# Two branch products in three fp32r passes, with group norm's factors applied ahead of its root

## The reference, cut to what matters

```python
# end of rwkv7_mix: group norm over 64 channels, weight, bias, bonus, gate
y = ((y - mean) * lax.rsqrt(var + GN_EPS)).reshape(B, S, RW_DIM)
y = y * gn_w + gn_b
bonus = jnp.sum(r_h * k_h * r_k, axis=-1, keepdims=True) * v_h
y_rw = (y + bonus.reshape(B, S, RW_DIM)) * g

# merge of the two branches, then the output projection
merged = gate_rw * (y_rw @ w_branch_rw) + gate_mla * (y_mla @ w_branch_mla)
x = x + merged @ w_out
```

## Time and profile before

| | |
|---|---|
| median of 3 runs | 2196.2 us (2192.58 to 2197.61) |
| the profiled execution | 2193.25 us |
| its span, first to last instruction | 2191.4 us |
| TensorE (PE) busy | 2140.6 us, 98% |
| VectorE (DVE) busy | 1323.2 us, 60% |
| ScalarE (ACT) busy | 950.8 us, 43% |
| mean granted TensorE clock | 0.991 |
| share of TensorE in the chain that ended last | 90% |

### The profile page before, as it was taken

How to read it: one execution, slowest core, us unless ns; L and a number is a source line. 1 busy time by engine, 2 the same in 40 slices (tenths; PEclk the granted TensorE clock), 3 DMA queues, 4 the chain that set the end, 5 groups by cost and what they waited for, 6 DMA issues and landing times.

```text
span 2191.4 us, 32956 instructions
## 1 busy us (share of the span) xinstructions
PE 2140.6 (98%) x13984; PEld 1677.7 (77%) x13984; DVE 1323.2 (60%) x1976; ACT 950.8 (43%) x1442; POOL 189.1 (9%) x159
## 2 busy tenths in 40 slices
PE   8999999999999999999999999999999998999997
PEld 6886788888888786888888875666888467777775
DVE  8887555245437877464255454767433454888887
ACT  5446533222334357422123332343222134888885
POOL 1230000000001310100000200000000010222220
PEclk9999999999999999999999999999999997999999
DMA  5222133322221230222222222111111343799985
GB/s 189 68 83 78 44 121 120 120 96 96 96 96 63 72 101 32 77 98 99 98 99 98 100 82 83 65 61 64 70 58 40 125 195 119 297 349 366 354 342 217
DMA packets 54999, 275.68 MB, mean 126 GB/s; under 512 B 13142, under 2 KB 13398, under 8 KB 26048
## 3 DMA queue, kind: packets, MB, share of 16 engines
q1 hardware_dynamic: 45344, 264.32, 33.3%
q0 software_dynamic: 8928, 8.33, 1.1%
q10 hardware_dynamic: 576, 0.87, 0.1%
HBM read 268.31 MB, written 29.36 MB: 136 GB/s over the span
## 4 chain that ended last, share of the span: by engine, by line
PE 90%; DVE 5%; ACT 2%; issue 1%; DMA 1%; POOL 0%; DVEq 0%; POOLq 0%; ACTq 0%
PE psum L123 87%; PE psum L126 3%; DVE A_mix L136 1%; ACT A_mix L130 1%; DVE WL L136 1%; DMA A_moe<-h_rows,A_moe 1%; DVE A_second L136 1%; DVE A_mix L156 0%; DVE A_second L144 0%; ACT WH L130 0%; ACT A_mix L133 0%; DVE A_mix L162 0%; DMA V<-in_vecs 0%; ACT R_moe L130 0%; ACT HH L130 0%
## 5 line engine op out<-in xcount | busy, mean ns | idle before, releaser
L136 DVE TENSOR_TENSOR WL<-raw,WH 128x1024 fp32r<-128x1024 f32 x236 | 300.6, 1276 | 351.2 <-ACT WH L130 350.7
L130 ACT ACTIVATE WH<-raw 128x1024 fp32r<-128x1024 f32 x236 | 247.3, 1054 | 348.8 <-PE psum L123 333.3
L123 PE MATMUL psum<-HH,WH 128*128 128x512 f32 x736 | 302.2, 411 | 17.5 <-DVE HL L144 10.1
L123 PE MATMUL psum<-R_op,WH 128*128 128x512 f32 x1024 | 316.2, 390 | 0.0
L123 PE MATMUL psum<-R_ffn,WH 128*128 128x512 f32 x1024 | 315.4, 389 | 0.0
L123 PE MATMUL psum<-HH,WL 128*128 128x512 f32 x736 | 290.2, 394 | 0.0
L123 PE MATMUL psum<-HL,WH 128*128 128x512 f32 x736 | 290.0, 394 | 0.0
L123 PEld LDWEIGHTS psum<-R_op,WH 128*128 128x128 f32 x1024 | 192.2, 188 | 40.9 <-issue 1.0
L123 PEld LDWEIGHTS psum<-R_ffn,WH 128*128 128x128 f32 x1024 | 192.2, 188 | 40.0
L123 PE MATMUL psum<-R_moe 128*128 128x512 f32 x800 | 199.0, 405 | 6.0 <-DVE ring_moe L136 3.6
L123 PE MATMUL psum<-R_ffn,WL 128*128 128x512 f32 x512 | 199.2, 389 | 0.0
(11 more groups left out here) (206 smaller groups left out, 2993.8 us busy)
## 6 DMA issues: line engine op xcount, KB each, us to landing
ring_moe<-in_w_gu SPq DMA_DIRECT2D x64, 1024.0 KB, 10.7
raw<-in_w_in SPq DMA_DIRECT2D x41, 1024.0 KB, 4.9
raw<-in_w_up SPq DMA_DIRECT2D x32, 1024.0 KB, 4.9
raw<-in_w_down SPq DMA_DIRECT2D x32, 1024.0 KB, 4.9
ring_moe<-in_w_dn SPq DMA_DIRECT2D x32, 1024.0 KB, 7.3
raw<-in_w_out SPq DMA_DIRECT2D x12, 1024.0 KB, 4.9
kept<-A_second SPq DMA_DIRECT2D x20, 256.0 KB, 2.2
A_mix<-A_mix SPq DMA_DIRECT2D x64, 64.0 KB, 2.0
```

Source lines behind the costliest of these rows:

```text
L123: return self.raw.matmul(o, l, r, start=start, stop=stop)
L130: return self.raw.activation(o, i, f, scale=scale)
L136: return self.raw.tensor_tensor(o, a, b, op)
```

## The change

Five things change, all in the second block's end.

1. The four branch weight chunks become split chunks, laid out in units of four kt blocks x 256 columns. `branch_mm` makes each product in three passes. The unsplit path (`wide_pe`) goes.
2. The branches' outputs are split: `parts_act` copies the eight tiles to `R_highs`, `parts_dve` subtracts into `R_lows`.
3. The weight units of the branches are split in new steps (`branch_act`, `latent_dve`, `mrg_act`, `mrg_dve`); the first two of them by the steps of the last gate projection.
4. Group norm's tail is written anew: (bias + bonus) x `gg` before the means are subtracted, y x weight x `gg` behind the squares, ahead of the reciprocal; after the reciprocal one multiply and one add per tile are left.
5. The latent branch's first two tiles stay in `TAB`, only two are parked and loaded again, into the buffers `keep` (so after the stores of the last gates out of them); `YM` goes.

```diff
-        s2.wm_c, s2.wr2_c = ([chunk(I["wb"][b, j], "raw") for j in range(2)] for b in (1, 0))
+        s2.wm_c, s2.wr2_c = ([chunk(I["wb"][b, j]) for j in range(2)] for b in (1, 0))
...
+            for j in range(4):
+                e.wait_ge(*at("rw_act", "gg", j))
+                e.stt(s2.bonus[:, j, :], s2.bonus[:, j, :], v("gnb", j), s2.gg[:, j, :], ADD, MUL).then_inc(
+                    *did("rw_dve", "bg", j))
...
+            for j in range(4):
+                e.wait_ge(*at("rw_act", "gq", j))
+                e.stt(s2.yrw[:, j, :], s2.yrw[:, j, :], v("gnw", j), s2.gg[:, j, :], MUL, MUL).then_inc(
+                    *did("rw_dve", "yg", j))
             turn.next()
             e.wait_ge(*at("rw_act", "gr"))
             e.recip(s2.grn, s2.grn).then_inc(*did("rw_dve", "grn"))
...
-                e.stt(y, y, v("gnw", j), b, MUL, MUL).then_inc(*read("rw_dve", turn, n))
+                e.tt(y, y, b, MUL).then_inc(*read("rw_dve", turn, n))
                 e.wait_ge(*last("rw_dve"))
-                step(e.stt(y, y, v("gnb", j), s2.bonus[:, j, :], ADD, ADD), "g2", j)
-                e.tt(y, y, s2.gg[:, j, :], MUL).then_inc(*did("rw_dve", "gn", j))
-                if j:
-                    yield
+                e.tt(y, y, s2.bonus[:, j, :], ADD).then_inc(*did("rw_dve", "gn", j))
+                yield
...
-        RWKV_DVE = filled(ORDER2 + "bcbc", g=33, b=8)
+        RWKV_ACT = filled(OPENING + "cccfccycy" + STATES + "cffcff" + "yybyyc", g=33, b=9)
+        RWKV_DVE = filled(OPENING + "cccfccyyc" + STATES + "cff" + "cbyfcyfycbycy", g=33, b=10)
...
+        def branch_mm(e, o, u, m, kt, hi, lo):
+
+            wh, wl = unit(u)
+            cs = slice(kt * 256 + m * 128, kt * 256 + (m + 1) * 128)
+            e.mm(o, wh[:, cs], hi[:, kt, :], kt == 0, False)
+            e.mm(o, wh[:, cs], lo[:, kt, :], False, False)
+            return e.mm(o, wl[:, cs], hi[:, kt, :], False, kt == 3)
...
+                    e.wait_ge(*at("parts_dve", "m", kt))
+                    t = branch_mm(e, bk(MB[i % 3]), u, i % 2, kt, s2.mh, s2.ml)
...
+                e.act(s2.mh[:, kt, :], s2.ym[kt], ACT.Copy).then_inc(*did("parts_act", "m", kt))
...
+                e.tt(s2.ml[:, kt, :], s2.ym[kt], s2.mh[:, kt, :].bitcast(F32), SUB).then_inc(*did("parts_dve", "m", kt))
...
         def mrg_pe(e):
+            us = s2.wr2_u
+            for kt in range(4):
+                e.wait_ge(*at("parts_dve", "r", kt))
                 for m in range(4):
...
+            e.wait_ge(*at("yk"))
+            for m in range(2):
+                e.wait_ge(*at(f"kept{m}", 7))
+                e.dma(s2.ym[2 + m], kept[2 + m]).then_inc(*sent("ym", m))
```

More of the change, by code:

```diff
@@ L263, in build @@
                 R_op.append(sb(st, f"R_op{i}", 16 * S, F32R))
+        with ExitStack() as st:
+            R_lows = sb(st, "R_lows", 8 * S, F32R)
+            sb(st, "between", 10 * S)
+            R_highs = sb(st, "R_highs", 8 * S, F32R)
         A_sec = phase("second", NA)[0]
@@ L456, in used @@
         def used(u):
-            l = lin_of_chunk[units[u][0]]
-            if units[u] == (l.chunks[-1], 1):
+            l = lin_of_chunk.get(units[u][0])
+            if l and units[u] == (l.chunks[-1], 1):
                 return at("lin_mm", l.n, 1)
@@ L2243, in wide_made @@
[L2243 to L2263, removed]
@@ L2280, in mrg_pe, with parts_dve @@
[L2280 to L2282 removed]
+                e.act(s2.rh[:, kt, :], s2.yrw[:, kt, :], ACT.Copy).then_inc(*did("parts_act", "r", kt))
+                yield
+        def parts_dve(e):
+            e.wait_ge(*at("rw_pe", 3, "tok", 1))
+            e.wait_ge(*at("rw_dve", "gp", 3))
+            for kt in range(4):
+                e.wait_ge(*at("parts_act", "m", kt))
+                e.tt(s2.ml[:, kt, :], s2.ym[kt], s2.mh[:, kt, :].bitcast(F32), SUB).then_inc(*did("parts_dve", "m", kt))
+                if kt % 2:
+                    yield
+            for kt in range(4):
+                e.wait_ge(*at("parts_act", "r", kt))
+                e.tt(s2.rl[:, kt, :], s2.yrw[:, kt, :], s2.rh[:, kt, :].bitcast(F32), SUB).then_inc(
+                    *did("parts_dve", "r", kt))
+                yield
@@ new lines, in branch_act, with latent_dve, made @@
+        def branch_act(e):
+            act_hi(e, s2.wm_u[2])
+            yield
+            yield
+            act_hi(e, s2.wm_u[3])
+            yield
+            yield
+            act_hi(e, s2.wr2_u[0])
+            yield
+            yield
+            act_hi(e, s2.wr2_u[1])
+            yield
+            yield
+            act_hi(e, s2.wr2_u[2])
+            yield
+        def latent_dve(e):
+            def made(i):
+                if i % 4 == 0:
+                    e.wait_ge(*at(f"kg{8 + i}"))
+                e.wait_ge(*branch_made("m", i))
+                e.tt(s2.gate[:, 8 + i, :], bk(MB[i % 3]), s2.gate[:, 8 + i, :], MUL).then_inc(*did("mrg_dve", "m", i))
+            dve_lo(e, s2.wm_u[2])
+            made(0)
+            yield
+            made(1)
+            yield
+            dve_lo(e, s2.wm_u[3])
+            made(2)
+            yield
+            made(3)
+            yield
+            dve_lo(e, s2.wr2_u[0])
+            made(4)
+            yield
+            made(5)
+            yield
+            dve_lo(e, s2.wr2_u[1])
+            yield
+            made(6)
+            yield
+            made(7)
+            yield
+            dve_lo(e, s2.wr2_u[2])
+            yield
```

118 lines of the change are left out of this document (67 added, 51 removed).

## The result

| | before | changed |
|---|---|---|
| median | 2196.9 us (2192.58 to 2197.63, 4 runs) | 2182.86 us (2177.18 to 2185.56, 4 runs) |
| the profiled execution | 2193.25 us | 2185.56 us |
| its span | 2191.4 us | 2183.6 us |
| TensorE busy | 2140.6 us | 2128.2 us |

The changed kernel takes 0.9939 of the time before (95% interval 0.9924 to 0.9955): 14.0 us less by the medians. The profiled execution is the slowest of the four.

A forecast was written before the change was run, and what follows sets the result against it. TensorE was taken to bound the kernel. A gain of 11.0 us less 0.5 and 0.2 lost gave 10.3, rounded to 10.2: 2183.0 from the profiled execution, 2186.0 from the median, middle 2184.5 us; range 2180.5 to 2190.5.

The forecast's parts named there:

- TensorE's work: Branch products in three passes instead of plain f32: gain 5.3 us in the latent branch, 5.7 in the recurrent, together 11.0.
- The reload, just hidden: Latent branch's first product: the reloaded tiles are copied and split just in time; 0 us lost, bounds 0 and 2.
- The recurrence: Low parts of weight units and a gate multiply ahead of state updates on VectorE make TensorE wait for nothing: 0 lost.
- The reciprocal behind the factors, 0.5 us lost at `gb`: Group norm's tail: VectorE's gate multiply and four factors start the reciprocal 2 us late; TensorE loses 0.5 us, bounds 0 and 1.5.
- Two splits late, 0.2 us lost: Entering the recurrent branch, the third and fourth splits of y come late on VectorE; 0.2 us lost, bounds 0 and 2.
- The merge: VectorE's merge work ends at 1766.9, the output projection wants its last low part at 1768.4: 1.5 us spare, 0 lost.
- The part behind as long as before (420.3 us): From the output projection to the end everything follows that projection, so the length stays 420.3 us and all gain is kept.
- one of my own signs of being wrong: The prediction called itself wrong if the output projection to the end was not as long as before, 420.3 us.
- VectorE as the pace (0.15): Rival, chance 0.15: VectorE's 17.6 us of new work sets the pace, tightest from 1728 to 1747; gain 7.5, 2187 us.
- A lower clock in the stretch: Rival, chance 0.03: waits for splits lower TensorE's clock in the recurrent branch; with all 96 passes +11.5 us, 2206.

The follow-up runs named there:

- the second time: The changed kernel run again without any edit; 2183.97 us median of 5 runs, ratio 0.9952 to the kernel before.
- The reordered queue: Changed kernel with the loads of the latent branch's two parked tiles issued behind the sixteen gate tiles on SP's queue, not ahead; 2197.08 us, one run.
- the old tail: Changed kernel with group norm's tail as before: no factors ahead, three operations per tile after the reciprocal; 2185.68 us median, ratio 0.9966 to the kernel before.
- the one extra low part: Changed kernel with one more 128x1024 subtraction (1.16 us) on VectorE ahead of the first split of y; 2185.05 us, one run.
- the factors behind the reciprocal: Changed kernel with the four factors (y x weight x gg) moved from ahead of the reciprocal to behind it; 2187.88 us, one run.
- the kernels with longer stretches: Overwritten extra products in the recurrent branch: 48 more passes in the changed kernel, 2192.18 us; two or five plain products in the kernel before, 2195.68 and 2201.72 us.
- the two-pass kernel: Changed kernel without the pass of high weights with low activations in both branches, low parts still computed; 2179.32 us, one run.
- the extra low parts: Changed kernel with one or three more 128x1024 subtractions on VectorE ahead of the first split of y; 2185.05 and 2187.7 us, one run each.

## Why the prediction was right

The forecast was 2184.5 us in a range of 2180.5 to 2190.5; 2182.86 and, the second time, 2183.97 were measured. The gain was forecast at 10.2 us, all of it in the stretch; the stretch gave 11.1 and 10.75.

- **TensorE's work**: right. 2.95 us per group alone (2.94 forecast), 21.76 us for the recurrent branch (21.8). Up to the recurrent branch 5.45 us were gained, waits included, where 5.3 were forecast without them. The rule that I weighed, 216 ns between matmuls of 512 columns (the Trainium skill, "TensorE: Matmul & The Clock Gate", Back-to-back issue gap, which gives it as the isolated gap), would have given an estimated 96 x 0.216 = 20.7 us for the recurrent branch; the trace does not agree, with 21.76, as the row had it.
- **The reload, just hidden**: right, with its bound. Not waited for in one profile, 0.3 us in the other, where ScalarE waited 1.45 us for the loads. The reordered queue shows what stood behind the estimate: 12.45 us.
- **The recurrence**: right, 0 lost.
- **The reciprocal behind the factors, 0.5 us lost at `gb`**: the mechanism is right, the size is not. It does start behind the four factors, but only 0.1 us is lost. The term mis-sized is 0.7 + 3.1 for a gate multiply and four factors. It measures 3.26 us (1730.75 to 1734.01): 0.61 for the multiply and 0.66 for each factor from start to start, though they are recorded with 0.69 and up to 0.75. The earlier trace rows had shown such a shorter distance for one kind (0.61), and I used the longer figures here. Where an operation uses the result of the one ahead, the distance is longer: 0.71 us (1743.20 to 1743.91), and 0.78 for a SCALAR_TENSOR_TENSOR in the old tail.
- **Two splits late, 0.2 us lost**: wrong by the same half a us. All four come early, by 0.4 us at the thinnest. That this place has the thinnest cover is right: 1.16 us more work there costs 1.0, and the old tail of the norm 2.1. One wait was not in my list at all: the fourth product needs the bank that a gate multiply frees. It was 0.9 us early, and it is the first to be waited for when VectorE is a us later (0.34 us, with the one extra low part and with the factors behind the reciprocal).
- **The merge**: right; VectorE's last split ends 6.5 us into the output projection (at 1772.3), just ahead of the 7.4 at which I had it wanted, and no wait shows. The cover is 0.9 us, where I had 1.5.
- **The part behind as long as before (420.3 us)**: this step was wrong, and it was one of my own signs of being wrong. It is 417.8 and 416.0 us. 1.75 us of that is the lower clock that did not come back at one place; the kernels with longer stretches show that the kind of product is not what brings it. The rest is within what the two profiles of the kernel before differ by (420.3 and 418.7). 11.1 or 10.75 and 1.75 make 12.5 to 12.9 us, between the two measured differences of the medians, 14.0 and 10.6. That the time itself came within 2 us of the forecast is in part luck: medians of the same kernel move by some us from one comparison to the next, and 2182.86 us would have fitted a gain of 12 as well as one of 10.

The rivals: VectorE as the pace (0.15) is not what happened, but both the two-pass kernel and the extra low parts show it half a us away. A lower clock in the stretch did not come in the changed kernel; behind a wait of 2.3 us it did, at a cost of 1.6 us. It stayed away with the waits of 1.02 and 0.70 us of the old tail and with one of 1.84 in the two-pass kernel.

## What to carry to other kernels

When a bound engine's work is cut, list what the next engine must have ready at each point where the first will come, by the distance from start to start and not by the recorded durations; here that settles whether the margin is -0.2 or +0.4 us. Count the buffers that it must free as well as the operands that it must make. Rewriting a chain off the critical path brings nothing by itself (0.0 us here), and may be worth something (2.1 us here) with the change that makes it critical, so try such edits together as well as apart. Compare the changed stretch in the profile and not the whole time alone: the stretch repeated to 0.4 us where whole executions differ by 5 to 10.

## What the runs showed of the hardware

- **The clock can fall without an idle gap.** TensorE was busy for the whole of the 42 to 46 us window in every kernel, and from the start of the output projection up to it. It is at the lower of its two levels there in five profiles (clock 0.50 to 0.70, distances nearly doubled) and at the full one in nine, with the same instructions. What it did just before is the run of 32 matmuls of 36 columns (3.65 us). At or behind the end of the second such run the clock was down to 0.50 in all fourteen profiles, 50 to 58 us behind the output projection's start. A change elsewhere that shifts the place by a few us can give or take 1.75 us. The Trainium skill ("TensorE: Matmul & The Clock Gate", HAM oscillation) has idle gaps bring the lower clock: the wait of 12.45 us did, and this trace agrees there, while the fall behind the routing came without a gap, which that section does not have.
- **Identical code drifts by us, in part by the clock.** The start of the stretch lay between 1702.6 and 1710.8 in the fourteen profiles, though TensorE's work ahead of it is the same in all. Between the first profiles of the two kernels it comes in steps. The first, 1.6 us, comes between 866 and 876 us; from 870 to 876 the mean granted clock was 1.00 before and 0.72 in the changed kernel. At another 128 matmuls of 64x64 took 6.61 us in the changed kernel's execution and 3.95 in the other; from 1520 to 1528 us the clocks were 0.58 and 1.00. Both places lie ahead of the change.
- **A long wait costs more than itself.** 2.3 us of waiting ahead of the recurrent branch left eight matmuls 0.43 us apart in place of 0.23, 1.6 us more; 12.45 us left some 2.8 more. A short wait costs 0.1 us more too: with the one extra low part the second matmul behind the wait starts 0.33 us after the first (1746.07 to 1746.40) in place of 0.23.
